# Softmax attention: logits two units ahead of the transposes, queries and keys in two buffers, turns written out; the last mixer head's scores ahead of the layer norm's sum

## The reference, cut to what matters

```python
proj = jnp.einsum('bsd,de->bse', h, w_in)
q, k, v, f_logit = jnp.split(proj, [D_MODEL, 2 * D_MODEL, 3 * D_MODEL], axis=-1)
q = heads(q) * (FOX_HEAD_DIM ** -0.5)
...
c = jnp.cumsum(log_f, axis=1).transpose(0, 2, 1)
def q_block(blk):
    logits = jnp.einsum('bhqd,bhkd->bhqk', qb, k).astype(jnp.float32)
    logits = logits + cb[:, :, :, None] - c[:, :, None, :]
    logits = jnp.where(q_pos[:, None] >= key_pos[None, :], logits, -jnp.inf)
    p = jax.nn.softmax(logits, axis=-1).astype(v.dtype)
    return jnp.einsum('bhqk,bhkd->bhqd', p, v)
```

```python
mu = jnp.mean(xf, axis=-1, keepdims=True)
var = jnp.mean(jnp.square(xf - mu), axis=-1, keepdims=True)
y = (xf - mu) * lax.rsqrt(var + EPS) * g + b
```

## Time and profile before

| what | us |
|---|---|
| median of the runs | 2437.01 |
| lowest and highest | 2432.64, 2437.63 |
| the profiled execution | 2438.1 |
| its span, first to last instruction | 2436.3 |
| PE busy | 2286.9 (94%) |
| POOL, DVE, ACT busy | 1481.2, 1165.5, 624.6 |
| the eight attention turns on PE, first L(0) to the output projection's rest | 941.64 to 1225.24, 283.60 |
| the mixer's last scores and first sum on PE | 380.75 to 387.52 |

### The profile page before, as it was taken

One profiled execution on the slowest core, in us unless ns is written; L12 is line 12 of the kernel. 1 busy time (PEld: TensorE's weight loads), 2 busy tenths in 40 slices (PEclk: granted clock), 3 DMA queues, 4 the chain that ended last, 5 costly groups with the idle time before them and its releaser, 6 DMA issues. The chain is left out here.

```text
span 2436.3 us, 28526 instructions
## 1 busy us (share of the span) xinstructions
PE 2286.9 (94%) x9952; PEld 1772.6 (73%) x9952; DVE 1165.5 (48%) x1942; ACT 624.6 (26%) x1077; POOL 1481.2 (61%) x704
## 2 busy tenths in 40 slices
PE   7899998989999998998999999998988979999997
PEld 4677775767887876666667887876777757888785
DVE  4878886974333015545443222008787854322102
ACT  2222334132221013332232111013444443111100
POOL 3756762648777885334278777885222218877784
PEclk9999999999999999999999999998999989999999
DMA  5222222722222322211023222331111112222232
GB/s 213 98 84 74 91 95 96 285 78 95 95 92 89 100 91 72 68 61 53 34 70 104 95 95 86 104 103 46 59 52 52 53 35 85 91 91 94 95 102 79
DMA packets 56501, 216.33 MB, mean 89 GB/s; under 512 B 6232, under 2 KB 6232, under 8 KB 53232
## 3 DMA queue, kind: packets, MB, share of 16 engines
q1 hardware_dynamic: 52992, 206.96, 24.8%
q10 hardware_dynamic: 3440, 8.44, 1.0%
HBM read 213.23 MB, written 2.15 MB: 88 GB/s over the span
## 5 line engine op out<-in xcount | busy, mean ns | idle before, releaser
L814 POOL TENSOR_TENSOR w_hi<-raw,ones 128x1024 fp32r<-128x1024 f32 x315 | 604.3, 1918 | 668.3 <-DMA raw<-in_wstream 667.5
L820 POOL TENSOR_TENSOR w_lo<-raw,w_hi 128x1024 fp32r<-128x1024 f32 x342 | 838.6, 2452 | 232.0 <-ACT w_hi L1543 207.3
L308 PE MATMUL ps<-u_hi,w_hi 128*128 128x512 f32 x1760 | 721.9, 410 | 14.4 <-DVE hv L2016 6.2
L308 PE MATMUL ps<-u_lo,w_hi 128*128 128x512 f32 x1760 | 701.4, 399 | 0.0
L308 PE MATMUL ps<-u_hi,w_lo 128*128 128x512 f32 x1760 | 700.6, 398 | 0.0
L308 PEld LDWEIGHTS ps<-u_hi,w_hi 128*128 128x128 f32 x1760 | 334.9, 190 | 94.4 <-DVE hv L2016 6.7
L308 PEld LDWEIGHTS ps<-u_hi,w_lo 128*128 128x128 f32 x1760 | 333.9, 190 | 82.1
L308 PEld LDWEIGHTS ps<-u_lo,w_hi 128*128 128x128 f32 x1760 | 335.0, 190 | 76.0 <-issue 3.1
L308 PE MATMUL ps<-f_hi,w_hi 128*128 128x512 f32 x528 | 210.9, 400 | 7.7 <-ACTq L85 7.7
L308 PE MATMUL ps<-f_lo,w_hi 128*128 128x512 f32 x528 | 210.2, 398 | 0.0
L308 PE MATMUL ps<-f_hi,w_lo 128*128 128x512 f32 x528 | 210.2, 398 | 0.0
(11 more groups left out here) (305 smaller groups left out, 2940.2 us busy)
## 6 DMA issues: line engine op xcount, KB each, us to landing
raw<-in_wstream SPq DMA_DIRECT2D x342, 512.0 KB, 3.4
ada_buf<-in_ada SPq DMA_DIRECT2D x16, 1024.0 KB, 5.7
ada_start<-in_ada SPq DMA_DIRECT2D x8, 1024.0 KB, 16.8
cbc<-decay_rows ACTq DMA_DIRECT2D x8, 512.0 KB, 3.5
x<-in_xT SPq DMA_DIRECT2D x1, 2048.0 KB, 8.1
bc<-gate_rows ACTq DMA_DIRECT2D x4, 512.0 KB, 5.1
out_T<-x ACTq DMA_DIRECT2D x8, 256.0 KB, 2.0
prm<-in_params SPq DMA_DIRECT2D x1, 357.5 KB, 2.8
```

The source lines that it names most:

```text
L308: last = nc.tensor.matmul(out, a, b, start=(start and k == 0 and i == 0), stop=(stop and k == nk - 1 and i == 2))
L814: g.tensor_tensor(w_hi[slot][:], raw[slot][:], ones[:, 0:1].to_broadcast([P, D]), ALU.mult).then_inc(chunk_hi, 1)
L820: g.tensor_tensor(w_lo[slot][:], raw[slot][:], w_hi[slot][:].bitcast(f32), ALU.subtract).then_inc(chunk_split, 1)
```

## The change

Four things change in the attention. **Logits two units ahead**: L(0) and L(1) are issued ahead of the first turn, and after every third step the hook issues T(n) and then L(n + 2); at n = 6 and 7 these are L(0) and L(1) of the next pair. DVE and ACT follow: N(n + 2), r, s(n + 2) and e(n + 2) stand beside pl(n) and ph(n). **Queries and keys twice**: q_hi, q_lo, k_hi, k_lo have two buffers, and DVE scales q and k after units 2 and 4, and makes q_lo and k_lo in units 3 and 5. `pr` moves to another place in SBUF to make room. **Places**: pv1 of the pair before goes from kk = 1 to kk = 3, the transposes of the values from kk = 4 to kk = 6. **Turns written out** on DVE and ACT, with constants in the waits, and one semaphore for each kind of step in the place of one for each engine. In the mixer, the last head's scores are issued ahead of the layer norm's first sum.

The number and the sizes of the matmuls, activations and vector operations stay as they are.

```diff
-        pe.wait_ge(v_cv[1].sem, v_cv[1].at("ys", H1 - 1))
+        att_scores_pe(H1 - 1)
+        pe.wait_ge(v_cv[1].sem, v_cv[1].at("ys", H1 - 1))
         p_ln.did(nc.tensor.matmul(ps[4][:], mean_w[:], acc[:], start=True, stop=True), "mu")
-        att_scores_pe(H1 - 1)
...
             def hook(kk):
-                if kk == 1:
-                    if lag:
-                        fox_weigh(i - 1, 1)
...
-                elif kk == 4:
+                if kk == 3:
+                    if i:
+                        fox_weigh(i - 1, 1)
+                elif kk == 6:
                     fox_values(i)
                 elif kk % 3 == 2:
                     n = kk // 3
-                    if n + 1 < U:
-                        fox_logits(i, n + 1)
                     fox_turn(i, n)
+                    if n + 2 < U:
+                        fox_logits(i, n + 2)
+                    elif i + 1 < PAIRS:
+                        fox_logits(i + 1, n + 2 - U)
                     if n == NT + 1:
                         fox_weigh(i, 0)
-            fox_logits(i, 0)
...
+        for i in range(PAIRS):
+            for n in range(U):
+                ahead = (i, n + 2) if n + 2 < U else (i + 1, n + 2 - U)
+                if ahead[0] < PAIRS:
+                    fox_negated(*ahead)
+                if i and n == 0:
+                    fox_rest(i - 1)
+                fox_prob_low(i, n)
+                if i + 1 < PAIRS and n in (3, 5):
+                    fox_low(i + 1, "ql" if n == 3 else "kl")
+                if ahead[0] < PAIRS:
+                    fox_divided(*ahead)
...
+                if i + 1 < PAIRS and n in (2, 4, U - 1):
+                    fox_scale(i + 1, {2: 0, 4: 1, U - 1: 2}[n])
```

More of the change, by code:

```diff
@@ L191, in build @@
     a_lo = place("a_lo", KT * T, f32r, [KT, T])
-    q_hi, q_lo, k_hi, k_lo = [place(n, T, f32r) for n in ("q_hi", "q_lo", "k_hi", "k_lo")]
+    q_hi, q_lo, k_hi, k_lo = [[place(f"{n}{b}", T, f32r) for b in range(2)] for n in ("q_hi", "q_lo", "k_hi", "k_lo")]
     fv = place("fv", T)
@@ L203, in build @@
     lg = [place(f"lg{i}", T) for i in range(2)]
+    pr = [place(f"pr{i}", T) for i in range(2)]
     assert here[0] <= mix_end
@@ new lines, in fox_round @@
+            act.wait_ge(v_proj.sem, v_proj.at(what + "s", i))
+            if what == "v":
+                if i:
+                    act.wait_ge(p_vT.sem, p_vT.at("vT", i - 1))
+            elif i >= 2:
+                act.wait_ge(p_L.sem, p_L.at(f"L{U - 1}", i - 2))
+            if what == "q":
+                ins = A(q_hi[i % 2][:], ps[0][:], ACT.Identity, scale=-float(FOX_D) ** -0.5)
+            else:
+                ins = A({"k": k_hi[i % 2], "v": fv}[what][:], ps[j][:], ACT.Identity)
@@ new lines, in fox_high, with fox_result @@
+        def fox_high(i, n):
+            a, r = divmod(n, NT)
+            act.wait_ge(p_T.sem, p_T.at(f"T{n}", i))
+            if i and n % NT == 0:
+                act.wait_ge(p_pv.sem, p_pv.at(f"pv{a}", i - 1))
+            a_ph.did(A(pt_hi[a][:, 0:r + 1, r * P:(r + 1) * P],
+                       ps[6 + n % 2][:, 0:(r + 1) * P].rearrange("p (s c) -> p s c", c=P), ACT.Identity), f"ph{n}")
+        def fox_result(i):
+            act.wait_ge(p_pv.sem, p_pv.at("pv1", i))
+            a_fox.did(A(a_hi[:, i, :], ps[3][:], ACT.Identity), "hi")
@@ new lines, in _ @@
+        fox_cbc(0)
+        for what in "qkv":
+            fox_round(0, what)
+        fox_expo(0, 0)
+        fox_expo(0, 1)
+        for i in range(PAIRS):
+            if i + 1 < PAIRS:
+                fox_cbc(i + 1)
+            for n in range(U):
+                if not (i and n == 0):
+                    fox_high(i, n)
+                if n + 2 < U:
+                    fox_expo(i, n + 2)
+                elif i + 1 < PAIRS:
+                    fox_expo(i + 1, n + 2 - U)
+                if i and n == 0:
+                    fox_result(i - 1)
+                    fox_high(i, n)
+                if n == 1:
+                    act.wait_ge(p_vT.sem, p_vT.at("vT", i))
+                    if i:
+                        act.wait_ge(p_pv.sem, p_pv.at("pv1", i - 1))
@@ L1478, in fox_result @@
-        def fox_result(i):
-            act.wait_ge(p_fox.sem, p_fox.at("pv1", i))
-            dst = a_hi[:, i - 1, :] if isinstance(i, int) else a_hi[:, bass.ds(i - 1, 1), :]
-            a_fox.did(A(dst, ps[3][:], ACT.Identity), "hi")
-        a_fox.open(act)
-        act.wait_ge(v_fg.sem, v_fg.at("zero_lo"))
-        PAIRS = FOX_H // 2
-        fox_act_turn(0, 0, lag=False)
-        with act.Fori(0, PAIRS // 2 - 1) as it:
-            for sub in range(2):
-                fox_act_turn(2 * it + sub + 1, 1 - sub)
```

315 lines of the change are left out of this document (120 added, 195 removed).

## The result

The changed kernel takes 2398.97 us (median of 4 runs, 2394.99 to 2400.91), the kernel before, measured beside it, 2437.32. The ratio is 0.9844, 95% interval 0.9829 to 0.9859. Measured again later beside two other kernels it took 2396.17 (5 runs, ratio 0.9839 [0.9821, 0.9857]). The forecast was 2395, with a range of 2385 to 2411.

What follows compares the result with a forecast made beforehand. PE, busy 94% of the span, was taken to bound the kernel. Idle time 27 + clock 11.8 + mixer 3.7 - 0.4 = 42.1 us off 2438.1 gives 2396.0; the median, 1.1 lower, is 2395 us, range 2385 to 2411.

Steps and rivals of the forecast that it cites:

- Two units ahead: Attention on PE: no transpose waits for `pr` any more, removing 14.4 + 0.9 = 15.3 us of idle time.
- the first rival: Attention, 0.17: one wait a turn stays, T 2.3 us late by an s 4.3 us longer, or k_lo late; 2410.
- Queries and keys earlier: Attention: logits no longer wait for k_lo, except the first wait of 7.8 us; 9.1 us removed.
- The idle time and the clock, 27 and 11.8: Eight attention turns: 27 us of PE idle time removed, and 11.8 us of busy time lost to low clock regained.
- The wait of the last turn for fv, 1.3, goes with it: Last attention turn: PE's 1.3 us wait for the scaled values disappears, v being scaled the turn before.
- pv1 in the last turn, 0.4: Last attention turn: no projection steps fill the place ahead of pv1, so 0.4 us is added.
- The mixer, 3.7: Mixer's end: scores run under the wait for `acc` and the squares start earlier; 3.7 us gained, upper bound 4.2.
- the clock stays low: Rival, 0.10: the attention's waits go, but the clock stays low as often; 2407.
- the signs that the forecast had named for its being wrong: New PE wait (a_hi, fv, pt_lo), s over 2 us ahead of transposes, or PEclk below 1 in turns without waits.
- DVE's wait for a_hi, which was to make it slower: Rival, 0.03: in the attention, DVE's wait for a_hi, up to 5.2 us before, becomes the bound; 2453.

Runs made afterwards that it cites:

- e3_vwait: Changed kernel with PE's last-turn waits for q_lo, k_lo and fv moved from the turn's head to just before the first output product: 2392.33 us, ratio 0.9815.
- e9_fill_klo: Kernel before, with 6 surplus matmuls ahead of the next pair's L(0), in the gap of the wait for k_lo: 2428.44 us, ratio 0.9974.
- the second pair of traces: The changed kernel and a copy of e3_vwait, measured again side by side: 2396.17 us for the changed kernel, 2395.8 us for the copy.
- e4_one_ahead: Changed kernel with logits one unit ahead instead of two, queries and keys still in two buffers: 2425.66 us, ratio 0.9952.
- e12_fill_t7: Kernel before, with four surplus matmuls ahead of T(7) alone, in the gap of the wait for `pr`: 2430.71 us, ratio 0.9964.
- e6_unroll: Kernel before, with the six middle turns of ACT and DVE written out in place of loops, nothing else: 2437.42 us, ratio 1.0004.
- e1_mixer: Kernel before with the mixer's edit alone, the last head's scores issued ahead of the first sum: 2433.33 us, ratio 0.998.

## Why the prediction was right

**Two units ahead.** Right, and the main step. No transpose waits for `pr`. Single steps of s are held up even longer than in before, 2.12 us (below) and 2.40 (at 939.07) at the longest, where before has 1.81. s(7) of the last turn but one, on DVE, with POOL beside it:

```profile
1141.98 2.12 DVE L1875 TENSOR_SCALAR pr<-pr,row_inv 128x512 f32<-128x512 f32 x1
...
1141.92 1.89 POOL L812 TENSOR_TENSOR w_hi<-raw,ones 128x1024 fp32r<-128x1024 f32 x1 [5.45 <-DMA raw<-in_wstream]
1143.89 2.45 POOL L818 TENSOR_TENSOR w_lo<-raw,w_hi 128x1024 fp32r<-128x1024 f32 x1
```

The 64 steps of s in the turns take 40.3 us, 0.63 in the mean; this one takes over three times as long, and PE doesn't wait, since two units stand between. The 47 steps that meet no instruction of POOL take 0.49 at most. The Trainium skill, "SBUF — State Buffer", section "Who interferes with whom", says that a `tensor_scalar` and GpSimd can hold each other up for a whole instruction. The rows agree: POOL's L812 starts 0.06 ahead of s(7), and s(7) ends 0.29 behind L812's end. It isn't held by L818 as well, so the 4.3 us more that the first rival had worked out from both instructions of POOL was not reached by any s.

**Queries and keys earlier.** Right: 7 of 8 waits for k_lo are gone. The runs add what the forecast had not parted: most of that comes of the order, and the second buffer is worth some 3 us by the traces.

**The idle time and the clock, 27 and 11.8.** In after the turns have 28.67 - 5.55 = 23.1 us less idle and 254.93 - 243.97 = 11.0 less busy time; in e3_vwait, without the last turn's wait, 26.0 and 12.5, together 38.5, beside 27 + 11.8 - 0.4 = 38.4 in the forecast. So the forecast fits the kernel that it described, and e3_vwait is that kernel; the changed one gives 34.1. (The waits that were to go are 16, 7 and 1, so 24 and not 22, and the upper bound 29.3; it changes nothing.) The fills size the clock by itself: e9_fill_klo has 42 surplus matmuls (1249 against 1207) of 0.233 us, the step from one projection matmul to the next, so without them PE is busy 253.00 - 9.8 = 243.2, which is 11.7 less than before. The reason given for it was too wide, though. "It is low here only in turns in which PE has stood idle three times" is so, but the first of the three waits does nothing: e9_fill_klo keeps those ahead of T(3) and has the clock up.

**The step that failed.** "The wait of the last turn for fv, 1.3, goes with it" did not come true: it is 3.3, and with its low stretch it costs 249.52 - 245.09 = 4.4 us, and 4.7 in the second pair of traces. PE's rows with a wait at the same place in before:

```profile
1183.31 0.66 PE L1069 MATMUL ps<-ident,pr 128*128 128x128 f32 x4 [0.95 <-DVE pr L1904]
1185.28 0.32 PE L1058 MATMUL ps<-k_hi,q_hi 64*128 64x128 f32 x1 [1.31 <-DVE k_lo L1869]
1187.31 0.76 PE L1080 MATMUL ps<-pt_hi,va_hi 128*128 128x512 f32 x1 [1.32 <-ACT fv L1418]
```

The three waits together are 3.58 us, and 3.33 is what is left of them in after. The change didn't make fv later: from the start of the turn's last projection matmul to fv's end it took 5.1 us in before (1181.97 to 1187.06) and 4.7 in after (1146.77 to 1151.43). The two waits ahead of it had only covered it, and once they were gone the whole of it showed. The forecast had v scaled "in the turn before", which is right for the code's order, but not early: v is the last of the three projections, DVE scales it behind N(1), pl(7) and s(1) at the turn's end, and the last turn has no projections for PE to do meanwhile. I looked where pv1 had moved and passed over where the wait itself stands; it is ahead of T(0), which doesn't need it. So in the sum the waits at that place were counted as gone, and at the head of the last turn they were not.

**pv1 in the last turn, 0.4.** Right: in e3_vwait the wait for pt_lo there is 0.41.

**The mixer, 3.7.** The mechanism was right and the size 0.5 low: from sum to squares 2.56 us for 6.77, 4.2, the upper bound of that step. The sum ran at full clock (1.13 us for 2.08), which the forecast counted only by half.

**The rest.** The kernel is 38.4 less by medians, where 42.1 was forecast: the turns' 34.1 and the mixer's 4.2 are 38.3, and what is missing is about the wait for fv. By the spans of the two profiled executions it is 43.1, with 4.8 outside both places. Executions of one kernel differ by as much (2431.49 to 2441.49 for nine runs of the kernel before), so this is not put down to the change. Of the rivals, "one wait a turn stays" did not come, nor did "the clock stays low": its four low stretches behind the turns' start have become one, behind the wait of 3.3. Of the signs that the forecast had named for its being wrong, two came. A wait for fv stands ahead of T(0), under the name "issue", and it is the step above. And steps of s of over 2 us appear, 2.12 and 2.40, but no transpose waits for them, so this sign was chosen too narrow. The new name pt_lo is no third one: its 0.8 is the wait of 1.4 of pv1 behind pl(7) at the end, which was listed under DVEq. DVE's wait for a_hi, which was to make it slower, is 3.1 us at the longest, where it was 5.2:

```profile
DVE a_lo L1889 <- ACT a_hi L1439: 20.9, 8, 3.1
```

## What to carry to other kernels

When the engine that bounds the kernel waits about 1 us at many places for a chain over two other engines, put one more unit of work between start and use (making the chain itself faster was not tried here). It was worth an estimated 20 of the 38 us, 27 against the changed kernel with one unit, and it also absorbs steps of the chain that take several times their usual length. Then read the first and the last turn by themselves: a wait written at a turn's head for all of its inputs costs nothing while there is other work, and its full length in the turn where there is none. Where the clock falls with the waits, fill the gaps once with surplus work: it takes one run and says how much of the time is clock, here 10 of the 38 us.

## What was not expected of the hardware

- The clock's loss depends on where the idle time lies more than on how much there is. The turns of e4_one_ahead have as much idle time as those of before (28.7 us), in 28 short waits for pr and one of 4.9, and PE is busy 7.4 us less; the only low stretch behind their start begins in the wait of 4.9.
- Which of several like gaps lowers the clock stays open: the same pair of waits did it at four turn ends of before (1043.06, 1079.65, 1148.57 and 1185.28) and not at three (975.67, 1009.28 and 1114.88), and in e12_fill_t7 one lone wait of 1.40 did, and five like it did not. In e6_unroll and e1_mixer, with the same waits on PE, it happens at other turn ends than in before. In e9_fill_klo waits of 1.04 and 1.41 stand 2.0 us apart behind the last output product (1208.83 and 1210.87), and the clock stays at 1.00 there.
- A low stretch can fall on the work behind an edit in one execution and not in another: the mixer's squares took 10.27 us in e1_mixer (granted clock 0.73) and 7.70 in after (1.00), which has the same edit. An edit of 4 us is read more surely from the start of the next step than from the end of the stage.
